# A mixture of experts inside one long kernel: the experts' results handed back to the tokens through memory, or kept on chip and summed by one-hot products

## What is computed

```python
expert_id = grp[:, None] * EXPERTS_PER_GROUP + top_idx
...
def expert_block(args):
    toks, e = args
    xb = t_pad[toks]
    return (jax.nn.silu(xb @ w1[e]) * (xb @ w3[e])) @ w2[e]
...
y_slots = y_slots.reshape(n_slots, D) * slot_gate[:, None]
y = jax.ops.segment_sum(y_slots, slot_tok, num_segments=N + 1)[:N]
```

## Time and profile before

| | |
|---|---|
| median of three runs | 2519.45 us |
| profiled execution | 2519.52 us |
| its span | 2518.2 us |
| PE busy | 2245.9 us (89%) |
| DVE busy | 944.8 us (38%) |
| ACT busy | 694.5 us (28%) |
| POOL busy | 113.4 us (5%) |
| DMA moved | 379.27 MB |
| granted TensorE clock, mean | 0.946 |

### The profile page before, as it was taken

How to read it: one execution, slowest core, us unless ns; L and a number is a source line. 1 busy time by engine, 2 the same in 40 slices (tenths; PEclk the granted TensorE clock), 3 DMA queues, 4 the chain that set the end, 5 groups by cost and what they waited for, 6 DMA issues and landing times.

```text
span 2518.2 us, 27633 instructions
## 1 busy us (share of the span) xinstructions
PE 2245.9 (89%) x11583; PEld 1656.4 (66%) x11583; DVE 944.8 (38%) x1726; ACT 694.5 (28%) x1172; POOL 113.4 (5%) x112
## 2 busy tenths in 40 slices
PE   5999798879877787599878889999989999899998
PEld 4876587763333333278656688888777767788886
DVE  3437464440000000233667454234431365442334
ACT  3323353311000000122336323133122363231331
POOL 2100000000000000000000000000000000000000
PEclk8999899989999999799979999999979999999999
DMA  4332242178999999722110223332132201322330
GB/s 164 101 132 76 88 150 67 28 301 341 427 426 428 427 427 428 300 100 70 33 51 1 84 84 100 101 94 91 51 130 67 84 18 34 101 95 90 100 100 34
DMA packets 109618, 379.27 MB, mean 151 GB/s; under 512 B 16369, under 2 KB 21873, under 8 KB 96689
## 3 DMA queue, kind: packets, MB, share of 16 engines
q1 hardware_dynamic: 104160, 366.34, 38.6%
q0 software_dynamic: 5328, 11.09, 1.3%
HBM read 373.08 MB, written 12.58 MB: 153 GB/s over the span
## 4 chain that ended last, share of the span: by engine, by line
PE 73%; DMA 15%; DVE 8%; ACT 3%; issue 1%; POOL 0%; SPq 0%; ACTq 0%; DVEq 0%; POOLq 0%
PE PB L447 52%; PE PB L1848 5%; PE PB L464 4%; PE PB L763 4%; PE PB L457 3%; PE PB L655 3%; DMA W_raw<-in_w_exp_down 3%; DMA R<-in_w_exp_down 1%; DMA Z<-in_w_exp_down 1%; DMA R<-in_w_exp_up 1%; DMA FH_raw<-in_w_exp_gate 1%; DMA Z<-in_w_exp_gate 1%; DMA Z<-in_w_exp_up 1%; DVE W L439 1%; DMA FL_raw<-in_w_exp_up 1%
## 5 line engine op out<-in xcount | busy, mean ns | idle before, releaser
L447 PE MATMUL PB<-W,FH 128*128 128x512 f32 (+1 forms) x1792 | 561.1, 395 | 27.2 <-DVE W L439 16.1
L439 DVE TENSOR_TENSOR W<-R,W 128x2048 fp32r<-128x2048 f32 (+1 forms) x128 | 291.1, 2276 | 680.5 <-ACT W L431 680.4
L431 ACT ACTIVATE W<-R 128x2048 fp32r<-128x2048 f32 (+1 forms) x128 | 243.1, 1902 | 679.0 <-PE PB L447 670.9
L447 PEld LDWEIGHTS PB<-W,FH 128*128 128x128 f32 x1792 | 334.2, 191 | 98.8 <-DVE W L439 18.2
L447 PE MATMUL PB<-W,hid 128*128 128x512 f32 x1536 | 350.0, 389 | 4.1 <-DVE W L439 3.3
L447 PE MATMUL PB<-W,FL 128*128 128x512 f32 (+1 forms) x896 | 350.1, 391 | 0.0
L447 PEld LDWEIGHTS PB<-W,hid 128*128 128x128 f32 x1536 | 288.0, 188 | 65.1 <-DVE W L439 4.2
L447 PE MATMUL PB<-FH,W 128*128 128x512 f32 (+1 forms) x1152 | 324.8, 367 | 0.0
L447 PEld LDWEIGHTS PB<-FH,W 128*128 128x128 f32 x1152 | 210.1, 191 | 34.7
L447 PE MATMUL PB<-FL,W 128*128 128x512 f32 (+1 forms) x576 | 211.6, 367 | 0.0
L447 PEld LDWEIGHTS PB<-W,FL 128*128 128x128 f32 x896 | 170.5, 190 | 35.4
(11 more groups left out here) (314 smaller groups left out, 2407.9 us busy)
## 6 DMA issues: line engine op xcount, KB each, us to landing
R<-in_mlp_w_up SPq DMA_DIRECT2D x32, 1024.0 KB, 5.3
R<-in_mlp_w_down SPq DMA_DIRECT2D x32, 1024.0 KB, 5.0
Z<-in_w_exp_gate SPq DMA_DIRECT2D x12, 2048.0 KB, 32.8
Z<-in_w_exp_up SPq DMA_DIRECT2D x11, 2048.0 KB, 34.7
R<-in_w_exp_up SPq DMA_DIRECT2D x11, 2048.0 KB, 34.0
W_raw<-in_w_exp_down SPq DMA_DIRECT2D x11, 2048.0 KB, 33.7
Z<-in_w_exp_down SPq DMA_DIRECT2D x10, 2048.0 KB, 34.2
R<-in_w_in SPq DMA_DIRECT2D x12, 1024.0 KB, 5.3
```

The lines of the kernel that those rows point to most:

```text
L431: k.A.e.activation(w.splits[w.split_of[u]][0][:, 0:m], w.rows(u), ACT.Copy).then_inc(*w.hi.tick(u))
L439: k.V.e.tensor_tensor(wl[:, 0:m], w.rows(u), wh[:, 0:m].bitcast(F32), ALU.subtract).then_inc(*w.lo.tick(u))
L447: ins = te.matmul(bank, l, r, start=(start and n == 0), stop=(stop and n == len(terms) - 1), skip_group_check=True)
```

## The change

- The rows of a pair that stand for no token are zeroed after each gather (`dve_clean`, DVE, 128 x 1024), and PE's `turn` waits for that instead of for the gather.
- The gates are put into slot order by 32 small matmuls (`pe_places(..., "gates", ...)`), which PE runs after the first gate product, and are multiplied on in the operation that writes `acts`. DVE writes the one-hot input of these matmuls at the router's end.
- The result of a pair is no longer scattered. ACT writes both halves as `y_hi` in the fp32r form that PE multiplies in one pass, DVE writes the remainder `y_lo`.
- DVE writes a one-hot matrix `stands` (128 rows x 512 tokens, `mark`); PE multiplies it with `y_hi` and `y_lo` (`give_back`, 16 matmuls of 128 x 512), and DVE adds the eight sums to `X` (`add`). This is done for pair n-2 behind turn(n+1) of step n.
- `scratch_y`, the 16 scatters, the four loads and the eight adds of line 2071 are gone; the branch has no wait for the last scatter ahead of it.
- The order of slots 5 and 7 is exchanged, and loads 7 and 8 wait until the first gather has landed. The last six loads use slots 0, 1, 2, 5, 6, 4 and not 0 to 5, so that slot 3 and the buffer of the first cut are free early: the first two tiles of the next projection are issued right behind load 95, and the first is cut before the last down product ends, the second right after the last pair's results.

```diff
@@ -324,26 +323,31 @@
         self.mh = sb("mh", [P, 32])
         self.stat = sb("stat", [P, 256])
         self.over_i = sb("over_i", [P, MORE + 1], I32)
-        self.tmp = [sb(f"tmp{i}", [P, D]) for i in range(2)]
+        def also(name, shape):
+
+            at = (nc.sbuf_base + 31) // 32 * 32
+            return sb(name, shape), nc.alloc_sbuf_tensor_at(name + "_r", shape, FR, offset=at)
+        rows = [also(f"tmp{i}", [P, D]) for i in range(2)]
+        self.tmp, (self.y_hi, self.y_lo) = [t for t, _ in rows], [t for _, t in rows]
         self.nsp = [sb(f"nsp{i}", [P, S]) for i in range(4)]
...
         units, self.start = weight_units(a)
         self.w = Stream(nc, "w", units, self.splits_of(len(units)), self.splits, self.R,
                         range(self.start["compress"], self.start["compress"] + 4))
         slots = [self.Z[:, 8192:12288], self.Z[:, 0:4096], self.Z[:, 4096:8192], raw[0][:], raw[1][:],
-                 wide[1][0][:], wide[0][0][:], self.FL_raw[:], self.FH_raw[:]]
+                 self.FL_raw[:], wide[0][0][:], wide[1][0][:], self.FH_raw[:]]
         self.eid = {}
-        self.x1 = Blocks(nc, "e", slots, NPAIR)
-        self.x2 = Blocks(nc, "o", slots[0:3], MORE // 2)
+        self.x1 = Blocks(nc, "e", slots, NPAIR, [0, 1, 2, 5, 6, 4])
...
     ve.tensor_tensor(k.s44, k.lg[:, :, 0:4], k.gm[:, :, 0:1].to_broadcast([P, 4, 4]),
                      ALU.subtract).then_inc(*k.dve_step.tick("router", "less"))
     ve.tensor_tensor(dr[:, 0:4], k.em[:, :, 1], k.em[:, :, 0], ALU.subtract).then_inc(*k.dve_step.tick("router", "apart"))
-    tokv = k.tokv.rearrange("p (m w) -> p m w", w=2)
-                         tokv[:, :, w:w + 1].to_broadcast([P, 8, 32]), ALU.mult)
+    dve_rows(k, "places", NPAIR, k.dve_step)
+    dve_clean(k, k.x1, 0)
     V.wait_ge(*k.pe_step.at("total"))
...
@@ -1733,16 +1735,32 @@
     V.settle(ve.reciprocal(dr[:, 4:8], dr[:, 4:8]))
     V.settle(ve.tensor_tensor(gate[:, 0, :], k.gg, dr[:, 4:8], ALU.mult))
     V.settle(ve.tensor_tensor(gate[:, 1, :], gate[:, 0, :], dr[:, 0:4], ALU.mult))
-
+
+def dve_rows(k, what, n, dve_step):
 
 
     V, ve = k.V, k.V.e
-    bank, low = k.banks[what,], k.wide.rearrange("p c i n -> p (c i n)")[:, 0:2 * n]
-    V.settle(ve.tensor_scalar(low, bank[:, 0:2 * n], -1.0, NOROW, ALU.mult, ALU.add))
-    cap = k.cap.rearrange("p (w n) -> p w n", w=2)[:, :, 0:n]
-    ve.tensor_tensor(rows, low.rearrange("p (w n) -> p w n", w=2), cap, ALU.min).then_inc(*dve_step.tick(what, "rows"))
+    low = k.wide.rearrange("p c i n -> p (c i n)")[:, 0:n]
+    V.settle(ve.tensor_scalar(low, k.banks[what,][:, 0:n], -1.0, NOROW, ALU.mult, ALU.add))
+    ve.tensor_tensor(k.rows_u[:, 0:n], low, k.cap[:, 0:n], ALU.min).then_inc(*dve_step.tick(what, "rows"))
+    ve.tensor_scalar(k.taken[:, 0:n], low, S - 0.5, None, ALU.is_lt)
+    for i in range(NT):
+        ins = ve.tensor_scalar(k.stands_for[:, 0:n, i], low, -128.0 * i, None, ALU.add)
+    V.settle(ins)
+
+
+def dve_gates(k, what, n, pe_step, dve_step):
+    k.V.wait_ge(*pe_step.at(what))
+    k.V.e.tensor_copy(k.row_gate[:, 0:n], k.banks[what,][:, 0:n]).then_inc(*dve_step.tick(what, "rows"))
+    k.V.wait_ge(*dve_step.at(what, "rows"))
+
+
+def dve_clean(k, x, n):
+    k.V.wait_ge(*x.gathered[n % 3].at(n))
+    k.V.e.tensor_scalar(k.xg[n % 3], k.xg[n % 3], k.taken[:, n:n + 1], None, ALU.mult).then_inc(*x.cleaned.tick(n))
 
 
...
@@ -1772,9 +1790,10 @@
     for i in range(NT):
         Y.wait_ge(*k.rowed.at("moe", i))
         Y.e.dma_start(k.hd[128 * i:128 * i + 128, :], k.xg[i % 3]).then_inc(*k.hd_out[i].tick())
-    for u in (5, 6, 7):
-        sp_load(k, x, u)
-    Y.wait_ge(*k.pe_step.at("router", 3))
+    sp_load(k, x, 5)
+    sp_load(k, x, 6)
+    Y.wait_ge(*x.gathered[0].at(0))
+    sp_load(k, x, 7)
     sp_load(k, x, 8)
 
...
-        self.slot_of = {load: u % len(slots) for u, load in enumerate(self.loads)}
+        order = [u % len(slots) for u in range(len(self.loads) - len(last))] + last
+        self.slot_of = dict(zip(self.loads, order))
+        self.prior = [max((w for w in range(u) if order[w] == order[u]), default=None) for u in range(len(order))]
         self.landed = [on(f"landed{c}", 16) for c in range(len(slots))]
         self.gathered = [on(f"gathered{c}", 16) for c in range(3)]
-        self.y_out = [on(f"y_out{c}", 16) for c in range(2)]
...
@@ -1811,9 +1833,8 @@
 def sp_load(k, x, u):
 
     which, n, side = x.loads[u]
-    L = len(x.slots)
-    if u >= L:
-        k.Y.wait_ge(*x.multiplied.at(*x.loads[u - L]))
+    if x.prior[u] is not None:
+        k.Y.wait_ge(*x.multiplied.at(*x.loads[x.prior[u]]))
...
@@ -1839,7 +1860,7 @@
     def product(n, which, lhs, rows, banks):
         for side in range(2):
...
@@ -1850,6 +1871,16 @@
                     if (half, c) == (len(banks) - 1, rows - 1):
                         ins.then_inc(*x.multiplied.tick(which, n, side))
 
+    def give_back(n):
+
+        T.wait_ge(*x.marked.at(n))
+        for i in range(NT):
+            for half in range(2):
+                T.wait_ge(*x.y_v.at(n, half))
+                bank, at = k.banks.take(T, ("sum", n, i, half), x.added.at(n, i, half)), slice(512 * half, 512 * half + 512)
+                to = k.stands[:, 128 * i:128 * i + 128]
+                group(T.e, bank[:], [(to, k.y_hi[:, at]), (to, k.y_lo[:, at])]).then_inc(*x.summed.tick(n, i, half))
+
     turn(0)
     for n in range(m + 1):
         if n < m:
@@ -1857,18 +1888,23 @@
             T.wait_ge(*x.fed_a.at(n))
             T.wait_ge(*x.fed_v.at(n))
             product(n, "gate", k.xT[n % 2], 8, [bank])
+        if n == 0 and x is k.x1:
+            pe_places(k, "gates", 1, NPAIR, k.pe_step, k.dve_step)
         if n:
             bank = k.banks.take(T, ("at", n - 1), x.at_out.at(n - 1))
             T.wait_ge(*x.acted.at(n - 1))
             flips(k, bank, [k.acts[(n - 1) % 2][:, c::4] for c in range(4)]).then_inc(*x.at_turned.tick(n - 1))
         if n + 1 < m:
             turn(n + 1)
+        if n >= 2:
+            give_back(n - 2)
         if n < m:
             product(n, "up", k.xT[n % 2], 8, [k.banks.take(T, ("up", n), x.acted.at(n))])
         if n:
-            banks = [k.banks.take(T, ("y", n - 1, half), (x.y_v if half else x.y_a).at(n - 1)) for half in range(2)]
+            banks = [k.banks.take(T, ("y", n - 1, half), x.y_v.at(n - 1, half)) for half in range(2)]
             T.wait_ge(*x.at_out.at(n - 1))
             product(n - 1, "down", k.aT[(n - 1) % 2], 4, banks)
+    give_back(m - 1)
 
 
...
@@ -1896,11 +1932,17 @@
             ae.activation(k.sig[n % 2], k.banks["gate", n][:], ACT.Silu).then_inc(*x.gated.tick(n))
         if n + 1 < m:
             feed(n + 1)
+        if x is k.x1 and n == m:
+            act_cut(k, k.start["after"])
         if n:
             A.wait_ge(*x.multiplied.at("down", n - 1, 1))
-            if n >= 3:
-                A.wait_ge(*x.y_out[(n - 1) % 2].at(n - 3))
-            ae.activation(k.ys[(n - 1) % 2][:, 0:512], k.banks["y", n - 1, 0][:], ACT.Copy).then_inc(*x.y_a.tick(n - 1))
+            if n >= 2:
+                A.wait_ge(*x.summed.at(n - 2, 3, 1))
+            for half in range(2):
+                ae.activation(k.y_hi[:, 512 * half:512 * half + 512], k.banks["y", n - 1, half][:],
+                              ACT.Copy).then_inc(*x.y_a.tick(n - 1, half))
+    if x is k.x1:
+        act_cut(k, k.start["after"] + 1)
 
 
 def dve_blocks(k, x):
...
+
+    def mark(n):
+
+        if n:
+            V.wait_ge(*x.summed.at(n - 1, 3, 1))
+        ve.tensor_tensor(k.stands[:].rearrange("p (i t) -> p i t", i=NT), k.iota.unsqueeze(1).to_broadcast([P, NT, P]),
+                         k.stands_for[:, n, :].unsqueeze(2).to_broadcast([P, NT, P]), ALU.is_equal).then_inc(
+            *x.marked.tick(n))
+
+    def add(n):
+        for i in range(NT):
+            for half in range(2):
+                xs = k.X[:, i, 512 * half:512 * half + 512]
+                V.wait_ge(*x.summed.at(n, i, half))
+                if n:
+                    V.wait_ge(*x.added.at(n - 1, i, half))
+                ve.tensor_tensor(xs, xs, k.banks["sum", n, i, half][:], ALU.add).then_inc(*x.added.tick(n, i, half))
     feed(0)
+    if x is k.x1:
+        dve_gates(k, "gates", NPAIR, k.pe_step, k.dve_step)
     for n in range(m + 1):
         if n + 1 < m:
+            dve_clean(k, x, n + 1)
             feed(n + 1)
+        if n >= 2:
+            mark(n - 2)
+            add(n - 2)
+        if x is k.x1 and n == m:
+            dve_cut(k, k.start["after"])
         if n < m:
             V.wait_ge(*x.gated.at(n))
             V.wait_ge(*x.multiplied.at("up", n, 1))
             if n >= 2:
                 V.wait_ge(*x.at_turned.at(n - 2))
-            ve.tensor_tensor(k.acts[n % 2], k.sig[n % 2], k.banks["up", n][:], ALU.mult).then_inc(*x.acted.tick(n))
-        if n:
-            V.wait_ge(*x.multiplied.at("down", n - 1, 1))
-            if n >= 3:
-                V.wait_ge(*x.y_out[(n - 1) % 2].at(n - 3))
```

(43 more changed lines are left out.)

115 lines of the change are left out of this document (56 added, 59 removed).

## The result

The changed kernel takes 2489.56 us (median of 4 runs, 2483.71 to 2490.82), the kernel before beside it 2519.47 us (2518.38 to 2520.15): 29.9 us less, ratio 0.9877, 95% interval 0.986 to 0.9894. Forecast were 2492.8 us and 26.7 us less. The span of the profiled execution fell from 2518.2 to 2489.2 us, the mean granted clock rose from 0.946 to 0.961, and the DMA engines moved 370.86 MB instead of 379.27. The last is the first thing to compare: the queue that GpSimd's indirect transfers use went from 11.09 to 6.83 MB, 4.26 MB for 16 scatters, and the other from 366.34 to 362.17, the reload of 4.2 MB. So the bytes left as the diff says.

A forecast was written before the change was run, and what follows sets the result against it. The DMA stream of the experts' weights was taken as the bound: its start, bytes and two ends count. -4.8 - 7.0 + 4.4 - 19.3 = -26.7 us from 2519.5 gives 2492.8 us; own range 2485 to 2500, 8 in 10 within 2484 to 2502.

The forecast's parts named there:

- start, G to the landing of load 14: From the first gather's issue (G): faster gather, first product 6.3 us earlier; net -4.8 us, bounds -8 and +2.6.
- stream, from there to L: Up to the last tile's landing (L): 14 scatters fewer, -7.0 us, bounds -4.5 and -9.
- last products, T - L: From L to the last product's end (T): sums of pair 14 delay down(15), +4.4 us, bounds 0 and +8.
- tail, T to the projection: From T to the next projection's first matmul: T + 14.5 instead of T + 33.8, -19.3 us, bounds -22.5 and -10.
- the hole: Start of the stream: second product waits behind gate matmuls, a copy and the second zeroing; about 1.5 us lost.
- I take 0.5 each: Stream: each scatter taken out saves 0.5 us, between 0.3 and an upper bound of 0.62 from its bytes.
- PE keeps 2.9 us per pair: Inside the stream: PE's chain takes 27.9 us per pair, the stream 30.8, so added PE work stays hidden.
- Branch 1: Tail: passing the branch ahead of the transposes and features was put at 1 us.
- the holding back: Rival, start: holding back loads 7 and 8 brings nothing, the slow gather being its own; 2500.2 us, chance 0.12.
- the slower tail: Rival, tail: branch, clock and engines in series put the projection at T + 24; 2502.3 us, chance 0.12.
- nothing out of the stream: Rival, stream: scatters' bytes filled gaps, so the -7.0 us are lost; 2499.8 us, chance 0.04.
- PE as the bound: Rival, between turn(n+1) and up(n): PE's chain per pair reaches 33.9 us, kernel slower at 2539 us, chance 0.04.

The follow-up runs named there:

- hold_off: The changed kernel with loads 7 and 8 issued right behind 5 and 6 again, not held back for the first gather; 2500.51 us.
- the two scatter kernels: The changed kernel with 15 unread scatters put back, each beside a gather (2500.86 us) or apart from it (2501.01 us).
- late_weights: The changed kernel with the last six loads taking slots in turn and both cuts of the next projection's weights behind the last additions; 2493.97 us.
- gates_early: The changed kernel with the gates' operations moved ahead of the first zeroing on DVE and the first transposes on PE; 2492.33 us.
- before_held: The kernel before the change, with only the holding back of loads 7 and 8 until the first gather landed; 2512.32 us.

## Why the prediction was right

By its own terms, with the two profiles (2518.2 - 2489.2 = 29.0 us):

| term | forecast | measured |
|---|---|---|
| ahead of G | 0 | +0.7 |
| start, G to the landing of load 14 | -4.8 | -4.2 |
| stream, from there to L | -7.0 | -12.5 |
| last products, T - L | +4.4 | +3.7 |
| tail, T to the projection | -19.3 | -18.8 |
| from there to the end | 0 | +2.0 |
| sum | -26.7 | -29.1 |

- **Start**: right, cause and size. Holding back won the first gather's 7.5 us, the hole gave 2 us back, and one gather of the stream now falls into this stretch, 0.7 us that the next term gets.
- **Stream**: the mechanism right, the term mis-sized, and outside its bounds (-4.5 to -9). "I take 0.5 each" failed: a scatter costs 0.75, 14 of them 10.5. With the gather that moved 0.7, 1.3 us are left that no experiment placed; 0.7 of them may be the spread of L - G between like kernels. The rows had held it: eight loads with 1.33 scatters and as many gathers took 2.4 us more than the loads' bytes, 0.9 for each transfer, and the prediction put most of it down to the gathers. In the changed kernel a load lands 4.89 us behind the one before it, and 0.65 to 0.69 later where a gather lies between. Nor was 0.62, the bytes, an upper bound: the packets' own time is 0.70.
- **Luck**: the sum missed by 2.4 us although the stream alone missed by 5.5. The five other terms missed by 3.1 us together, all but the last products' towards less gain, and covered over half of it.
- **PE**: 27.64 us per pair against 27.9, the sum matmul 0.226 us against 0.227, the wait for the mark 18.0 us in 13, 1.4 each, as forecast. Right that it is hidden. "PE keeps 2.9 us per pair" was 2.4, and the first pairs need all of it to catch up; 8 more matmuls, which that account would have hidden, moved the end.
- **Last products**: +3.7 for +4.4, and +5.3 where the clock fell behind the idle 1.9 us.
- **Tail**: right within 0.5 us. "Branch 1" was wrong in itself: PE's branch took 5.9 us, 3.2 of them behind its sums. But these 3.2 lay beside DVE's last additions and its second cut, which ended at T + 7.1 and T + 9.3 (6.9 and 9.2 forecast); what the projection waited for in the end were transposes at half the clock and the features behind them.
- **After the projection's start** the changed kernel is 2 us slower, and all nine kernels built on it are slower too (1443.5 to 1448.5 against 1441.7 and 1442.7). In all ten a stretch at the low clock (0.5) near 390 us behind the start of the projection is 14 us long, and 10 in the two others; that can be a part of it. What causes it was not tried.
- Of the rivals, the holding back (0.12), the slower tail (0.12) and nothing out of the stream (0.04) are refuted by `hold_off`, by T + 15.0 and by the two scatter kernels. PE as the bound (0.04) did not come true, but 8 matmuls per pair would have brought it.

The Trainium skill ("DMA: Bandwidth & Descriptors", Queues, rings and completion order) has the DMA engines take turns between queues, so that the gather would not have to stand behind all of SP's loads. `hold_off` against the changed kernel is the measurement: 10.91 us with the loads queued, 3.51 without. A queue of its own did not get the gather past 2 MB loads that were already handed over, and the prediction was right to go by the rows.

## What to carry to other kernels

A transfer that the start of a stage hangs on is worth an empty DMA queue: two loads that were issued some 15 us later, once that transfer had landed (at 564 us and not at 549), won 7 to 8 us, and they were not missed. A result that goes through memory only to be gathered again costs more than its bytes, at both ends of the stage above all; here 16 matmuls per pair replace it, and cost nothing inside the stream as long as PE's chain stays shorter than the stream's; at its end they cost the last products 3.7 us. Measure that cover by adding work until the time moves, not from the busy share: PE, 88% busy in the stream, could not take 1.8 us more per pair for nothing.

## What the runs showed of the hardware

- An indirect transfer of 65 rows of 4 KB in a full stream costs the other transfers 0.67 us as a gather and 0.75 as a scatter, and a gather 1.3 us behind a scatter no more than one that is 7 us behind. It lands 10 to 12 us after its issue, a gather right behind a scatter in the same queue 14 to 16 us.
- After some 2 us of idle time PE's granted clock sometimes fell to half (0.5) for the next 3 us or so. Ahead of the sums of pair 14 PE idled 1.94 us in the changed kernel, `late_weights`, `gates_early` and `hold_off`; the 16 matmuls then took 3.94, 3.96, 5.51 and 5.54 us. This alone moves T by 1.6 us between kernels whose code is the same at that place.
- A branch whose block is skipped took PE's queue 5.9 us in the changed kernel, 4.2 to 6.0 in those built on it and 3.4 and 3.7 in `before` and `before_held`; 3.2 us of it stood between PE's last sum and its next transpose. Loading its flag early won PE 0.1 us and DVE 1.0. In `late_weights` DVE's branch took 0.07 us and ended at 1033.2, and yet the first operation behind it started only at 1037.1, with nothing that the profile shows to wait for.
